# A three-block model on one core: products of few rows in column groups, tables behind the first projection, one more weight slot

## The reference

```python
mod = jax.nn.silu(c) @ w_mod[l] + b_mod[l]          # one row of 1024 times 1024 x 6144
shift1, scale1, gate1, shift2, scale2, gate2 = jnp.split(mod[:, None, :], N_MOD, axis=-1)
h = rms_norm(x, g_pre_mix[l]) * (1.0 + scale1) + shift1
y = hybrid_mixer(h, w_in[l], w_gate_lr[l], b_gate[l], g_gla[l], w_out[l])
x = x + gate1 * rms_norm(y, g_post_mix[l])
h = rms_norm(x, g_pre_ffn[l]) * (1.0 + scale2) + shift2
y = moe_ffn(h, router_w[l], router_b[l], w_gate_up[l], b_gate_up[l], w_down[l], b_down[l])
x = x + gate2 * rms_norm(y, g_post_ffn[l])

# in hybrid_mixer: attention and gated linear attention (GLA) from one projection
q_a, k_a, v_a, q_g, k_g, v_g, r_g, g_lr = jnp.split(h @ w_in, split_points, axis=-1)
gate_logit = g_lr @ w_gate_lr + b_gate               # g_lr has 16 columns

# in moe_ffn: 32 experts, the 4 best of each token
gu = xb @ w_gate_up[e] + b_gate_up[e]                # 1024 x 2048 an expert
x_glu, x_lin = jnp.minimum(gu[:, ::2], 7.0), jnp.clip(gu[:, 1::2], -7.0, 7.0)
out = x_glu * jax.nn.sigmoid(1.702 * x_glu) * (x_lin + 1.0) @ w_down[e] + b_down[e]

# in odd_mixer of the third block: 8 input gates and 8 forget gates
qk, v, og, gates = jnp.split(h @ w_in, [2 * C_QK, 2 * C_QK + C_V, 2 * C_QK + 2 * C_V], axis=-1)
gates = gates + gate_b
```

## Time and profile before

| | us |
|---|---|
| median of 3 runs | 2490.14 |
| the runs | 2490.63, 2485.43, 2490.14 |
| the profiled execution | 2491.03 |
| its span, first to last instruction | 2488.6 |
| PE busy | 2259.7 (91%) |
| DVE busy | 872.5 (35%) |
| ACT busy | 414.8 (17%) |
| granted TensorE clock, mean | 0.963 |
| DMA | 657.11 MB, 264 GB/s in the mean |

### The profile page before, as it was taken

The page is one execution under the profiler, slowest core; times in us unless marked ns, Lnnn a source line. Parts: engine busy times, 40 slices in busy tenths (PEclk is TensorE's granted clock), DMA queues, the critical chain, the costliest instruction groups (busy, mean ns, idle before and its releaser), DMA issues. The chain is left out here.

```text
span 2488.6 us, 24986 instructions
## 1 busy us (share of the span) xinstructions
PE 2259.7 (91%) x9708; PEld 1295.1 (52%) x9708; DVE 872.5 (35%) x1795; ACT 414.8 (17%) x893; POOL 106.9 (4%) x74
## 2 busy tenths in 40 slices
PE   7999999988899888888869999998799999989998
PEld 4554443333333333333337688665558754547873
DVE  5675222211122121212137437645657201343201
ACT  1213110111111111111121322012321001222100
POOL 1000000000001000000000000001100000000000
PEclk8999999999999999999989999999999999999999
DMA  9766498999989999999978722664157443323441
GB/s 333 279 239 237 188 359 318 412 412 413 404 308 413 412 412 412 412 412 412 412 291 297 274 89 85 236 230 176 68 184 258 167 152 136 135 102 127 153 159 44
DMA packets 212411, 657.11 MB, mean 264 GB/s; under 512 B 8542, under 2 KB 13206, under 8 KB 195572
## 3 DMA queue, kind: packets, MB, share of 16 engines
q1 hardware_dynamic: 208528, 649.53, 68.4%
q0 software_dynamic: 1712, 3.60, 0.4%
q10 hardware_dynamic: 2004, 1.67, 0.2%
HBM read 653.72 MB, written 1.05 MB: 263 GB/s over the span
## 5 line engine op out<-in xcount | busy, mean ns | idle before, releaser
L1604 PE MATMUL ps<-w,XE 128*64 128x512 f32 x1152 | 338.6, 614 | 32.3 <-DMA w<-in_w_gate_up 20.5
L812 PE MATMUL ps<-HF,w 128*128 128x256 f32 x1408 | 309.5, 383 | 1.8 <-DVE CF L3040 1.8
L812 PEld LDWEIGHTS ps<-HF,w 128*128 128x128 f32 x1408 | 270.2, 192 | 41.6 <-issue 4.5
L1634 DVE TENSOR_TENSOR T<-ps,BB 128x512 f32<-128x512 f32 x64 | 44.3, 692 | 599.5 <-PE ps L1604 599.5
L1604 PEld LDWEIGHTS ps<-w,XE 128*64 128x64 f32 x1152 | 108.9, 141 | 194.7 <-issue 193.5
L1675 PE MATMUL ps<-w,AT 128*64 128x512 f32 x608 | 166.4, 601 | 24.4 <-DMA w<-in_w_down 16.4
L812 PE MATMUL ps<-HT,w 128*128 128x256 f32 x768 | 174.7, 385 | 5.0 <-DVE dqk L2390 2.4
L630 DVE SCALAR_TENSOR_TENSOR AUX<-w,CS,AUX 128x512 f32<-128x512 f32 (+1 forms) x228 | 169.8, 745 | 8.1
L812 PEld LDWEIGHTS ps<-HT,w 128*128 128x128 f32 x768 | 146.0, 193 | 27.7 <-issue 7.5
L828 PE MATMUL ps<-w,AF 128*128 128x512 f32 x352 | 151.6, 593 | 1.8 <-DVE AF L3062 1.8
L1604 PE MATMUL ps<-tables,XE 128*64 128x512 f32 x304 | 141.7, 621 | 9.1 <-DMA w<-in_w_gate_up 7.8
(11 more groups left out here) (587 smaller groups left out, 2644.2 us busy)
## 6 DMA issues: line engine op xcount, KB each, us to landing
w<-in_w_gate_up SPq DMA_DIRECT2D x72, 2048.0 KB, 20.5
w<-in_w_down SPq DMA_DIRECT2D x38, 2048.0 KB, 21.7
w<-in_ada_w SPq DMA_DIRECT2D x24, 2048.0 KB, 8.2
w<-in_ffn_w_in SPq DMA_DIRECT2D x20, 2048.0 KB, 8.0
tables<-in_w_gate_up SPq DMA_DIRECT2D x19, 2048.0 KB, 21.7
GR<-in_w_gate_up SPq DMA_DIRECT2D x19, 2048.0 KB, 18.2
AUX<-in_w_gate_up SPq DMA_DIRECT2D x18, 2048.0 KB, 20.5
w<-in_w_in SPq DMA_DIRECT2D x17, 2048.0 KB, 10.0
```

The costliest lines, as they stand in the source:

```text
L812: ins = e.matmul(out_, w[:, k, c:c + n], HT[:, k, :], start=k == 0, stop=k == kc - 1, skip_group_check=True)
L1604: ins = e.matmul(b[j * n:j * n + n, :], FM.XE[:, side(x), 4 * kh + k, j * n:j * n + n], ring.tile(512, 1024, "gu", ex_, h, kh, x[0])[:, k, ...
L1634: e.tensor_tensor(FM.T1[:, :], bank(x, "gu", q), FM.BB[:, q * 512:q * 512 + 512], ADD).then_inc(*dve())
```

## The change

Four edits go together.

1. `quarters_pe` runs a product of few output rows as eight matmuls that write to four different groups of 32 output rows: matmul k goes to rows 32 (k mod 4) and on, and the two that share a group add up. The result is in four parts, which a later step adds. For the conditioning, `ada_part_dve` copies the bank out and `ada_rows_sum_pe` sums the partitions by four matmuls of one column. It is used for ada 1, 2, 3, 12, 13, 14 and 15 (2 and 14 went to DVE before, 3 was split), each in one piece; for `glr` with 32 padded rows (the second matrix `wlr` is laid at four places in place of one, and the product with it adds the parts); and for the gates of the odd layer, with four copies by DVE and two matmuls with a selecting matrix `SELQ` after the first eight feature matmuls. The spread vector has one column of 32 set, the others cleared at the start.
2. The tables are loaded behind q1, and the waits for them go to DVE's rope, ACT's `qT` and PE's attention.
3. The MoE has an eighth slot `w7`, open after the attention, and uses it first.
4. The memory for the descriptors of POOL's software DMA goes from 16384 to 2048 (`dynamic_dma_scratch_size`).

```diff
-        self.turn, self.k = new[2:] + turn + new[:2], 0
+        self.turn, self.k = new[:1:-1] + turn + new[:2], 0
...
-        f.glr, f.wlr = (sb(x, [16, 256], c=ph) for x in ("glr", "wlr"))
+        f.glr, f.wlr = (sb(x, [128, 256], c=ph) for x in ("glr", "wlr"))
...
+        m.SLOTS.append(sb("w7", [128, 4096], c=ph)[:, :])
...
-    GLRW = GR[:, 2, 0:128].rearrange("p (k n) -> p k n", k=8)
-    CSB, TURN = GR[:, 3, :].rearrange("p (k q) -> p k q", k=8), GR[:, 2, 128:256]
+    GLRW = GR[:, 2, 0:256].rearrange("p (k n) -> p k n", k=8)
+    CSB = GR[:, 3, 0:256].rearrange("p (k q) -> p k q", k=8)
+    PART = {1: GR[:, 2, 512:1024], 2: GR[:, 1, 0:512], 3: GR[:, 1, 512:1024], 12: GR[:, 2, 512:1024], 13: GR[:, 4, 512:1024],
+            14: GR[:, 4, 0:512], 15: m.moe.T1[:, :]}
...
-        e.wait_ge(sems["consts_landed"], 32)
...
-        ada_sum_pe(e, 2)
-        ada_rows_pe(e, 3, CSB, n_cols=256)
-        b = bank.take(e, "ada", "3b")
-        e.wait_ge(*at("ada acc", 3))
-        for f in range(2, 4):
-            ins = e.matmul(b[:, f:f + 1], AC2[:, 0, cols(f)], ones[:, 0:1], start=True, stop=True, skip_group_check=True)
-        ins.then_inc(*pe("ada summed", 3))
+        ada_rows_sum_pe(e, 1)
+        for n in (2, 3):
+            ada_rows_pe(e, n, CSB)
+            ada_rows_sum_pe(e, n)
...
+        ada_part_dve(e, 1)
+        e.tensor_reduce(m.SELQ[:, :], ident.rearrange("p (g c) -> p c g", g=4)[:, 0:16, :], AX.X, ADD).then_inc(*dve())
+        ada_put_dve(e, 0)
+        ada_put_dve(e, 1)
+        ada_part_dve(e, 2)
+        ada_put_dve(e, 2)
         dve.name("first", "half mod")
         own(e, dve)
         first_put_dve(e, 2)
-        ada_acc_dve(e, 3, lo=256)
+        ada_part_dve(e, 3)
         ada_put_dve(e, 3)
...
-    BY_ROWS = (1, 3, 12, 13, 15)
+    BY_ROWS = (1, 2, 3, 12, 13, 14, 15)
...
-    def ada_rows_pe(e, n, spread, ks=range(8), n_cols=512):
+    def quarters_pe(e, b, n, lhs, rhs):
+
+        for k in range(8):
+            q = 32 * (k % 4)
+            ins = e.matmul(b[q:q + n], lhs(k), rhs(k), start=k < 4, stop=k >= 4, skip_group_check=True)
+        return ins
+
+    def ada_rows_pe(e, n, spread):
 
         w = ring.tile(1024, 512, "ada", n)
-        if ks[0] == 0:
-            bank.take(e, "ada", n, hold=True)
-            e.wait_ge(*at("w", "ada", n))
-        for k in ks:
-            ins = e.matmul(bank("ada", n)[:, 0:n_cols], spread[:, k, :], w[:, k, 0:n_cols], start=k == 0, stop=k == 7,
-                           skip_group_check=True)
-        if ks[-1] == 7:
-            ins.then_inc(*pe("ada rows", n))
-            if n_cols == 512:
-                pe.name("ada summed", n)
-            pe.leave("w", "ada", n)
-            bank.drop("ada", n)
-
-    def ada_turn_dve(e, n, fs):
+        b = bank.take(e, "ada rows", n)
+        e.wait_ge(*at("w", "ada", n))
+        quarters_pe(e, b, 32, lambda k: spread[:, k, :], lambda k: w[:, k, :]).then_inc(*pe("ada rows", n))
+        pe.leave("w", "ada", n)
+
+    def ada_part_dve(e, n):
 
         e.wait_ge(*at("ada rows", n))
-        for f in fs:
-            e.tensor_tensor_reduce(TURN if n < 15 else m.moe.T2[:, 0:128], bank("ada", n)[:, cols(f)], ident, 1.0, 0.0, MUL, ADD, st[:, 50 + f:51 + f]).then_inc(
-                *dve())
-            own(e, dve)
-        dve.leave("bank", "ada", n)
+        e.tensor_copy(PART[n], bank("ada rows", n)).then_inc(*dve("ada part", n))
+        dve.leave("bank", "ada rows", n)
+
+    def ada_rows_sum_pe(e, n):
+
+        b = bank.take(e, "ada", n)
+        e.wait_ge(*at("ada part", n))
+        for f in range(4):
+            ins = e.matmul(b[:, f:f + 1], PART[n][:, cols(f)], ones[:, 0:1], start=True, stop=True, skip_group_check=True)
+        ins.then_inc(*pe("ada summed", n))
...
+        tables_sync(e)
...
+        for q in range(0, 128, 32):
+            e.dma_start(F1.wlr[q:q + 16, :], T["w_gate_lr"][0]).then_inc(sems["gate_lr_landed"], 16)
...
-            ada_rows_pe(e, 12, CSB, range(4))
+            ada_rows_pe(e, 12, CSB)
             e.wait_ge(*at("att1 turned", "out", 0))
             e.wait_ge(*at("w", "out1", 0))
         if s in (6, 7):
             out1_pe(e, 0, s - 6, 0)
         if s == 8:
-            ada_rows_pe(e, 12, CSB, range(4, 8))
+            ada_rows_sum_pe(e, 12)
...
-        feat_pe(e, b[0:16, 0:256], GLRW, 0, 16, F1.HT).then_inc(*pe("glr"))
+        quarters_pe(e, b[:, 0:256], 32, lambda k: GLRW[:, k, :], lambda k: F1.HT[:, k, :]).then_inc(*pe("glr"))
...
-        ada_rows_pe(e, 13, CSB, range(4))
+        ada_rows_pe(e, 13, CSB)
+        ada_rows_pe(e, 14, CSB)
         e.wait_ge(*at("hn1", 0, "out"))
         turn_half_pe(e, "gla turned", 0, 512)
-        ada_rows_pe(e, 13, CSB, range(4, 8))
+        ada_rows_sum_pe(e, 13)
+        ada_rows_sum_pe(e, 14)
...
-        ada_sum_pe(e, 14)
         out1_pe(e, 1, 1, 1)
         norm_turn_pe(e, m.moe, "moe", 0)
         e.wait_ge(*at("spread", "again"))
-        ada_rows_pe(e, 15, CSB2, range(4))
+        ada_rows_pe(e, 15, CSB2)
         norm_turn_pe(e, m.moe, "moe", 1)
-        ada_rows_pe(e, 15, CSB2, (4, 5))
...
+    def tables_sync(e):
         e.dma_start(CT[:, 256:], T["consts"][:, 256:]).then_inc(sems["consts_landed"], 16)
...
-        ring.use(7)
-        opened = {4: at("rows used"), 5: at("rows used"), 6: at("gla", "out", 1)}
+        ring.use(8)
+        opened = {4: at("rows used"), 5: at("rows used"), 6: at("gla", "out", 1), 7: at("att1", "o", 1)}
...
-        ada_rows_pe(e, 15, CSB2, (7,))
+        ada_rows_sum_pe(e, 15)
...
+    def odd_gates_pe(e):
+        b = bank.take(e, "gates")
+        e.wait_ge(*at("gate parts", "out"))
+        for g in range(2):
+            ins = e.matmul(b[0:8, 256 * g:256 * g + 256], m.SELQ[:, 8 * g:8 * g + 8], FO.GP[:, :], start=True, stop=True,
+                           skip_group_check=True)
+        ins.then_inc(*pe("ogates"))
+
     def odd_pe(e):
         features(e, "odd")
         w = ring.tile(1024, 16, "gates")
         e.wait_ge(*at("w", "gates"))
-        b = bank.take(e, "gates")
-        for g in range(2):
-            ins = feat_pe(e, b[0:8, 256 * g:256 * g + 256], w, 8 * g, 8, FO.HT)
-        ins.then_inc(*pe("ogates"))
+        b = bank.take(e, "gate parts")
+        quarters_pe(e, b[:, 0:256], 16, lambda k: w[:, k, :], lambda k: FO.HT[:, k, :]).then_inc(*pe("gate parts"))
         pe.leave("w", "gates")
-        feats_pe(e, ("oqk", 0), ("oqk", 0), ring.tile(1024, 512, "oqk", 0), 4, FO.HT)
+        feats_pe(e, ("oqk", 0), ("oqk", 0), ring.tile(1024, 512, "oqk", 0), 4, FO.HT, odd_gates_pe)
...
+        e.wait_ge(*at("gate parts"))
+        e.wait_ge(*at("gate parts", "cleared"))
+        for q in range(0, 128, 32):
+            e.tensor_copy(FO.GP[q:q + 16, :], bank("gate parts")[q:q + 16, 0:256]).then_inc(*dve("gate parts", "out"))
+        dve.leave("bank", "gate parts")
...
-    nc = bacc.Bacc("TRN2", target_bir_lowering=False, num_devices=1)
+    nc = bacc.Bacc("TRN2", target_bir_lowering=False, num_devices=1, dynamic_dma_scratch_size=2048)
```

58 lines of the change are left out of this document (30 added, 28 removed).

## The result

The changed kernel takes 2478.2 us in the median of its runs, against 2489.86 for the kernel before on the same chip: ratio 0.9947, interval 0.9935 to 0.9959. That is 11.7 us faster where 27 were forecast. Five of its six runs lie between 2475.05 and 2479.43; the sixth took 8360.56, for a cause that no trace shows, and is left out of the ratio. The profiled execution took 2479.43 (span 2477.6).

A forecast was written before the change was run, and what follows sets the result against it. The MoE was taken as DMA-bound with two PE-bound islands, the rest as bound by PE and its waits. 12.5 + 10.5 + 4.7 = 27.7 us off 2491.03 gave 2463, range 2450 to 2478.

The forecast's parts named there:

- The start: From the beginning to q1: column groups and q1 loaded ahead of the tables gain 6.5 us, bounds 4 and 9.
- The slot: MoE: an eighth slot saves one load of 5.09 us per PE-bound island, two islands; 10.5 us, bounds 0 and 12.
- The odd gates: Odd layer: gates in four column groups gain 4.7 us, bounds 3 and 6.
- the sum: Whole program: gains of 12.5, 10.5 and 4.7 add to 27.7 us off the profiled 2491.03.
- The tail: End of the first stage, rows 13 to 15 in column groups: 5 us gained, bounds 2 and 7.
- the 12.5: First stage: start 6.5, attention 2.2 and tail 5 make 13.7 us, carried as 12.5 because of waits for ACT or DVE.
- the 3.3 us for rows 13 and 14 and for the norm's first transposes: Tail: 1.9 us from shorter rows 13 and 14, 1.4 from the MoE norm's transposes getting their bank earlier.
- the 1.8 us for the piece of rows 15: Tail: the piece of rows 15 right before the router, 1.88 us long, counts as 1.8 us gained.
- Attention: Rows 12 at attention: the second half becomes a sum of 0.5; 2.2 us gained, bounds 0 and 3.1.
- So it does in the stages behind: MoE and the stages behind it: the first stage's earlier start goes through one to one.
- rival 2: Start stays bound by landings and the clock; first stage gives 5 us, total 2471; chance 0.15.
- Rivals 1, 3 and 4: 1: slot gives nothing, 2474, chance 0.12; 3: four groups not parallel, 2472 or 2488, 0.08; 4: POOL DMAs late, 2555, 0.04.

The follow-up runs named there:

- tables_front: The changed kernel with the tables loaded ahead of q1 as before: 2479.77 us, ratio 0.9956.
- slot_late: The kernel before with the eighth slot alone (small descriptor memory, slot used last of the new ones, open after rows 15): 2484.19 us, ratio 0.9971.
- odd_only: The kernel before with only the gates of the odd layer in four column groups: 2490.2 us, ratio 0.9999.
- odd_fill: The changed kernel with four idle matmuls in the second half of the mLSTM, where PE waits for ACT: 2475.45 us, ratio 0.9938.
- The fillers: The changed kernel with twelve idle matmuls in PE's waits at the end of the first stage: 2475.98 us, ratio 0.9939.
- wide_tail: The changed kernel with rows 12 to 15 wide as before, 14 on DVE, and the eighth slot used later: 2469.33 us, ratio 0.9918.
- no_slot: The changed kernel with seven MoE slots in the former turn: 2487.05 us, ratio 0.9986.
- scratch_only: The kernel before with 2048 bytes of descriptor memory for POOL's software DMA in place of 16384: 2491.12 us, ratio 1.0001.

## Why the prediction was wrong

**The start: right, the exact number by luck.** 6.5 us was taken and 6.4 measured at q1, 6.1 at k1. The way there differed: q1 isn't held by its load, as PE meets ada 2 late (transposes and sums at half the clock). The 3 us taken off for the clock were put on the gate product and on q1, and it was these earlier steps that lost them. In other profiles with this start the transposes take 1.94 us at the full clock for 3.42 here, and over the eleven profiles with it (without tables_front) q1 begins at 38.9 to 42.4, where it stood at 47.4 to 48.4. Four groups do go side by side: 1.92 us of the 1.75 taken, including the end of the last record. The 2.3 us worked out from the Trainium skill ("TensorE: Matmul & The Clock Gate", "Part 3: Packing small matmuls — row/col tiling") is not borne out by these rows.

**The slot: right, in its mechanism too.** 10.5 us was taken. The MoE is 9.1 us shorter in the profile, and the profiles of eight slots take 1027.1 to 1032.2, those of seven 1037.2 to 1042.5. The changed kernel's first profile has the longest of the ten with eight slots (the others 1027.1 to 1029.4), so what it lacks there lies in that profile and not in the slot. slot_late shows the two steps of one load each.

**The odd gates: right at their place, wrong behind it.** 4.7 us was taken and 4.6 measured, and then the rest of the program takes 1.7 us longer (370.4 for 368.8), in odd_only 4.3. The failing step is the sum, which carries the 4.7 to the end of the span and puts what stands behind the gates at nothing: the lower clock falls on the output gate there. odd_fill shows that it is the clock.

**The tail: wrong.** "Sum of the tail 5, bounds 2 and 7" was the failed step, with the 12.5 carried from it. From the first GLA matmul to the first expert the changed kernel loses 2.8 us instead. By the rows above it is 7.8 us ahead at the output projection (189.47 and 181.72), 8.7 at the first norm transposes (217.09 and 208.36), 8.5 at the router, 5.7 at the ranks (231.89 and 226.22), 6.0 at the gather and 5.0 at the first expert. So three terms failed:

- Of the 3.3 us for rows 13 and 14 and for the norm's first transposes 1.0 came. The transposes of GLA's result take the bank that DVE frees behind the two new copies (1.24 us of idle); I costed the copies on DVE as free and didn't ask what stands behind them. And the first output projection runs in part at half the clock (1.8 us).
- Of the 1.8 us for the piece of rows 15 ahead of the router nothing came: PE now waits 1.62 us for DVE's last features there.
- The router at half the clock loses 2.8 us net. The lower bound of 2 named that very cause, "with less to fill its waits, PE may see the lower clock for longer", and priced it too small.

The gather's 5.49 for 4.54 is no mark of the change: in the other seven profiles with wide rows it takes 5.5 to 6.5. The router is one: it takes 3.73 in all eight profiles with the wide rows and 6.8 to 7.0 in the five with the narrow ones and no other edit there. From the first GLA matmul to the first expert it is 67.4 to 68.4 us in those eight, though their rows hold some 7 us more of PE's time, and 69.5 to 70.2 in these five. The fillers show that the router's loss is the clock, and wide_tail that the wide rows bring the tail back to 68.2. Attention gained 1.4 of the 2.2 taken.

**"So it does in the stages behind": wrong.** Between the MoE and the odd layer 5.4 us are lost in code that didn't change. Some of it is the profile of before, whose 791.9 is the shortest of all. In seven profiles of kernels with one part or two, or none, of the change these stages take 791.9 to 796.6, in nine of kernels with start, odd gates and the eighth slot's memory 796.4 to 799.1. The two groups touch, and their medians differ by 3.1 us (794.7 and 797.8). PE's clock is lower for longer there: 1.3 us stand at the product with HF, where no profile of the one group reaches the other. Why the whole brings this when none of the parts and pairs that were run does stays open.

In sum, of the 27.7 us 7.5 went at the first stage (12.5 taken, 5.0 measured), 1.4 at the slot, 0.7 between the MoE's last scatter and its norm, 5.4 in the untouched stages and 1.7 behind the gates, which leaves the 11.0 of the span. Each is a difference of one profile from another; the ratios of the two runs of the changed kernel, 0.9947 both, are firmer than the parts. No rival named this: rival 2 had the clock and the 5 us that the first stage gave, but it put the loss at the start, where 6.4 us came, and left the later stages as they were. Rivals 1, 3 and 4 are refuted by no_slot, by the 1.92 us, and by scratch_only.

## What to carry to other kernels

Matmuls that stand in PE's waits for other engines aren't free to remove: where PE waits and the rest of a chain runs through it, shorter products can cost more than they save, and each such place has to be looked at for the granted clock behind it. Use a faster form of a product where PE has work behind it, and keep the slow form where it fills a wait. When an instruction is put on another engine, look at which buffers that engine frees behind it. And a gain at one place is worth what is left of it at the end of the span: compare the starts of the same instruction down the whole program.

## What the hardware showed that was not expected

- 66 us behind the odd gates, with the same instructions around it, the lower clock came in all ten profiles with the quick gates and no fillers, and in none of the six others (7.13 us for 16 records, against 8.56 to 10.17).
- The lower clock can repeat its places from kernel to kernel and execution to execution: from the odd gates to the end, the eight profiles with 25.5 or 25.6 us of gates and no fillers there take 370.4 to 370.5 us, although they arrive there up to 16 us apart (2101.8 in wide_tail, 2117.6 in no_slot).
